# Attention scores of a fused trunk: the product of the rotated queries with the low part of the rotated keys on 64 rows of the array, two key banks from different row halves

## What is computed

```python
def mla_attend(q_n, q_r, k_n, k_r, v):
    s = jnp.einsum('bqhd,bkhd->bhqk', q_n, k_n) + jnp.einsum('bqhr,bkr->bhqk', q_r, k_r)
    p = jax.nn.softmax(s.astype(jnp.float32) * MLA_SCALE, axis=-1)
    return jnp.einsum('bhqk,bkhd->bqhd', p.astype(v.dtype), v)
...
    qr_l = apply_rope(qr_l, cos[:, None, :], sin[:, None, :])
    ...
    y_lat = (o_lat * jax.nn.silu(s_lat[3])) @ w_out
```

## Time and profile before

| | us |
|---|---|
| median of three runs | 3075.17 |
| lowest and highest | 3072.52, 3076.87 |
| the profiled execution's own time | 3071.61 |
| its span (first to last instruction) | 3069.8 |
| TensorE busy in it | 2917.5 (95%) |
| attention stage, from its first loads to its last matmul | about 1869 to 2857 |

### The profile page before, as it was taken

How to read it: one execution, slowest core, us unless ns; L and a number is a source line. 1 busy time by engine, 2 the same in 40 slices (tenths; PEclk the granted TensorE clock), 3 DMA queues, 4 the chain that set the end, 5 groups by cost and what they waited for, 6 DMA issues and landing times. The chain is left out here.

```text
span 3069.8 us, 38485 instructions
## 1 busy us (share of the span) xinstructions
PE 2917.5 (95%) x15623; PEld 2505.9 (82%) x15623; DVE 1531.2 (50%) x2791; ACT 1178.5 (38%) x1971; POOL 234.9 (8%) x275
## 2 busy tenths in 40 slices
PE   7999999999999999979979997999999999999798
PEld 7788888888888788857867886888888888887577
DVE  2625652654365535544432323666666656665353
ACT  2423322331233123322234222666666666665310
POOL 0100000000000000002320000202102012020000
PEclk8899999999999999989989998999999999999799
DMA  6311131113111311153341221000100101100432
GB/s 187 93 33 44 45 114 30 44 52 107 30 46 50 107 30 52 33 204 108 121 146 39 90 96 46 26 28 26 32 25 26 36 18 32 31 19 18 175 110 69
DMA packets 223866, 200.79 MB, mean 65 GB/s; under 512 B 12141, under 2 KB 194301, under 8 KB 223690
## 3 DMA queue, kind: packets, MB, share of 16 engines
q1 hardware_dynamic: 207194, 171.28, 18.5%
q0 software_dynamic: 4656, 16.56, 1.4%
q10 hardware_dynamic: 11840, 10.49, 1.0%
HBM read 157.34 MB, written 40.95 MB: 65 GB/s over the span
## 5 line engine op out<-in xcount | busy, mean ns | idle before, releaser
L40 PE MATMUL v_pj<-e_u_hi,e_w_hi 128*128 128x512 f32 (+1 forms) x864 | 308.7, 357 | 1.9 <-PEq L57 1.9
L40 PE MATMUL v_pj<-e_u_hi,v_w_hi 128*128 128x512 f32 (+1 forms) x864 | 308.6, 357 | 0.0
L41 PE MATMUL v_pj<-e_u_lo,v_w_hi 128*128 128x512 f32 (+1 forms) x864 | 306.7, 355 | 0.0
L41 PE MATMUL v_pj<-e_u_lo,e_w_hi 128*128 128x512 f32 (+1 forms) x864 | 306.7, 355 | 0.0
L42 PE MATMUL v_pj<-e_u_hi,v_w_lo 128*128 128x512 f32 (+1 forms) x864 | 306.5, 355 | 0.0
L42 PE MATMUL v_pj<-e_u_hi,e_w_lo 128*128 128x512 f32 (+1 forms) x864 | 306.5, 355 | 0.0
L40 PE MATMUL o_y_bank<-o_w_hi,o_m_hi 128*128 128x512 f32 x576 | 230.9, 401 | 48.8 <-DVE o_w_lo L1218 31.2
L1840 ACT CAST t_pt_hi<-t_ring 128x512 fp32r<-128x512 f32 (+1 forms) x384 | 181.6, 519 | 237.3 <-PE t_ring L2024 237.3
L1925 DVE TENSOR_TENSOR t_pt_lo<-t_ring,t_pt_hi 128x512 fp32r<-128x512 f32 (+1 forms) x384 | 216.2, 598 | 52.8 <-ACT t_pt_hi L1840 51.4
L41 PE MATMUL o_y_bank<-o_w_lo,o_m_hi 128*128 128x512 f32 x576 | 229.0, 398 | 0.0
L42 PE MATMUL o_y_bank<-o_w_hi,o_m_lo 128*128 128x512 f32 x576 | 228.6, 397 | 0.0
(11 more groups left out here) (380 smaller groups left out, 6446.5 us busy)
## 6 DMA issues: line engine op xcount, KB each, us to landing
e_w_raw<-in_ev_w_in SPq DMA_DIRECT2D x72, 512.0 KB, 4.7
v_mw<-in_mod_w SPq DMA_DIRECT2D x32, 512.0 KB, 4.3
l_w_raw<-in_od_w_in SPq DMA_DIRECT2D x21, 512.0 KB, 4.0
o_m_raw<-mixT SPq DMA_DIRECT2D x20, 512.0 KB, 5.3
m_w<-in_mod_w SPq DMA_DIRECT2D x16, 512.0 KB, 7.7
o_w_raw<-in_ev_w_out SPq DMA_DIRECT2D x16, 512.0 KB, 10.3
zgT<-l_lat_q POOLq DMA_DIRECT2D x16, 512.0 KB, 3.6
t_zg<-zgT SPq DMA_DIRECT2D x32, 256.0 KB, 2.7
```

Of the source, the lines that this page charges most:

```text
L40: nc.tensor.matmul(out, whi, xhi, start=first, stop=False)
L41: nc.tensor.matmul(out, whi, xlo, start=False, stop=False)
```

## The change

It does four things.

1. In `scores` the matmul with `kr2[1]` no longer takes 128 rows. It takes the high half alone, 64 rows; low x low is left out. Bank 1 takes it from rows (64 to 127) and banks 2 and 0 from rows 0 to 63. The three matmuls stand together behind bank 1's other four: bank 2, bank 1, bank 0 (the last with `start`, so that bank 0's four other matmuls add to it).
2. The high part must then lie in both row halves. A new tile `qx` holds a copy in the half that `qs` doesn't have it in. GpSimd makes the copy (`other_half`, 64 x 1024) in t = 5 of the head before, and for head 0 ahead of the slots; TensorE waits for it (`qx_ok`) in t = 0 of each head, just ahead of these three matmuls.
3. `zg` is one tile instead of two. The second half's gates are loaded when the first half's store has landed, and the next head's first half when the second's has.
4. `part` is no tile of its own but the first 512 columns of `w_raw`; the load of an even head's key weights into `w_raw` also waits for the turned queries (`turn_ok`).

```diff
         qs = [s.sb(f"qs{b}", [P, LAT], F32R) for b in range(2)]
+        qx = s.sb("qx", [P, LAT], F32R)
...
-        zg = [s.sb(f"zg{x}", [P, 512]) for x in range(2)]
-        turn, part = s.sb("turn", [P, LAT]), s.sb("part", [P, 512])
+        zg = s.sb("zg", [P, 512])
+        turn, part = s.sb("turn", [P, LAT]), w_raw[:, 0:512]
...
                 if n > 4:
                     sp.wait_ge(w_ok, n - 1)
+                    if (kind, h % 2) == ("k", 0):
+                        sp.wait_ge(turn_ok, h)
...
-                if h + 1 < AH:
-                    sp.wait_ge(og_out[x], 16 * (h + 1))
-                    gates(h + 1, x)
+                if (h, x) != (AH - 1, 1):
+                    sp.wait_ge(og_out, 16 * (2 * h + x + 1))
+                    gates(h + x, 1 - x)
...
+            def other_half(h):
+                r = DR * (h % 2)
+                o = DR - r
+                pool.wait_ge(qs_hi_ok, h + 1)
+                pool.tensor_copy(qx[o:o + DR, :], f(qs[h % 2][r:r + DR, :])).then_inc(qx_ok, 1)
+
             add(0, 0)
             add(0, 1)
+            other_half(0)
             for h, t in slots:
                 for op in projections(h, t):
                     if op[0] == "qr":
                         add(op[1], op[2])
+                if t == 5 and h + 1 < AH:
+                    other_half(h + 1)
...
+                hi_rows = [slice(DR * g, DR * g + DR) for g in range(2)]
+                high = [(qs[b] if g == b else qx)[hi_rows[g], tok] for g in range(2)]
+
+                def rope_low(j, g):
+                    k0, n = KEYS[j]
+                    return nc.tensor.matmul(S[:, k0:k0 + n], high[g], kr2[1][hi_rows[g], k0:k0 + n], start=j == 0, stop=j != 0)
+
                 for j in SCORE_ORDER:
                     k0, n = KEYS[j]
                     out = S[:, k0:k0 + n]
-                    mm3(nc, out, (qn[b][0][:, tok], qn[b][1][:, tok]), (kn[b][0][:, k0:k0 + n], kn[b][1][:, k0:k0 + n]), True, False)
-                    nc.tensor.matmul(out, qs[b][:, tok], kr2[0][:, k0:k0 + n], start=False, stop=False)
-                    last = nc.tensor.matmul(out, qs[b][:, tok], kr2[1][:, k0:k0 + n], start=False, stop=True)
+                    mm3(nc, out, (qn[b][0][:, tok], qn[b][1][:, tok]), (kn[b][0][:, k0:k0 + n], kn[b][1][:, k0:k0 + n]), j != 0, False)
+                    last = nc.tensor.matmul(out, qs[b][:, tok], kr2[0][:, k0:k0 + n], start=False, stop=j == 0)
                     if j == 1:
-                        last.then_inc(qk_part, 1)
+                        if t == 0:
+                            pe.wait_ge(qx_ok, h + 1)
+                        rope_low(2, 0)
+                        rope_low(1, 1).then_inc(qk_part, 1)
+                        rope_low(0, 0)
                 last.then_inc(qk_done, 1)
```

More of the change, by code:

```diff
@@ L1702, in stage_attend @@
             "qk_part", "qk_done", "most_ok", "bias_ok", "exp_ok", "rec_ok", "prob_ok"))
-        rope_part, rope_own = s.sem("rope_part"), s.sem("rope_own")
+        rope_part, rope_own, qx_ok = s.sem("rope_part"), s.sem("rope_own"), s.sem("qx_ok")
         turn_ok, qs_hi_ok, qs_ok = s.sem("turn_ok"), s.sem("qs_hi_ok"), s.sem("qs_ok")
-        zg_in, og_out = [s.sem(f"zg_in{x}") for x in range(2)], [s.sem(f"og_out{x}") for x in range(2)]
+        zg_in, og_out = s.sem("zg_in"), s.sem("og_out")
         wq_src = a["od_w_uq"].rearrange("a (k p) n -> p (a k) n", p=P)
@@ L1760, in gates @@
             def gates(h, x):
-                sp.dma_start(zg[x][:, :], zg_src[h * P:h * P + P, 512 * x:512 * x + 512]).then_inc(zg_in[x], 16)
+                sp.dma_start(zg[:, :], zg_src[h * P:h * P + P, 512 * x:512 * x + 512]).then_inc(zg_in, 16)
             def store(h, x):
                 sp.wait_ge(ring_free, at[("PV", h, x)])
-                sp.dma_start(og_dst[h * P:h * P + P, 512 * x:512 * x + 512], zg[x][:, :]).then_inc(og_out[x], 16)
-                if h + 1 < AH:
-                    sp.wait_ge(og_out[x], 16 * (h + 1))
-                    gates(h + 1, x)
+                sp.dma_start(og_dst[h * P:h * P + P, 512 * x:512 * x + 512], zg[:, :]).then_inc(og_out, 16)
+                if (h, x) != (AH - 1, 1):
+                    sp.wait_ge(og_out, 16 * (2 * h + x + 1))
+                    gates(h + x, 1 - x)
             for kind, h in LOADS[:4]:
@@ L1772, in _ @@
             gates(0, 0)
-            gates(0, 1)
             for h, t in slots:
@@ L1782, in _ @@
             store(AH - 1, 1)
-            for x in range(2):
-                sp.wait_ge(og_out[x], 16 * AH)
+            sp.wait_ge(og_out, 16 * 2 * AH)
         @block.gpsimd
@@ L1915, in low @@
                     dve.wait_ge(ring_done, at[op])
-                    dve.wait_ge(zg_in[x], 16 * (h + 1))
-                    nc.vector.scalar_tensor_tensor(zg[x][:, :], ps[:, :], 0.5, zg[x][:, :], ALU.mult, ALU.mult).then_inc(ring_free, frees(op))
+                    dve.wait_ge(zg_in, 16 * (2 * h + x + 1))
+                    nc.vector.scalar_tensor_tensor(zg[:, :], ps[:, :], 0.5, zg[:, :], ALU.mult, ALU.mult).then_inc(ring_free, frees(op))
                 else:
```

## The result

The changed kernel takes 3090.99 us in the median of 4 runs (3089.47 to 3096.77). The kernel before takes 3074.06 us beside it (4 runs, 3072.52 to 3076.87). The ratio is 1.0058, with a 95% interval of 1.004 to 1.0075: slower by 16.9 us, by more than the 0.2% that a measurement here can tell. The forecast was 3088.0 with a range of 3071 to 3120, and slower at 0.70. The profiled execution has a span of 3087.7 us, 17.9 over the 3069.8 of before.

The account below looks back on a forecast made before the run. The prediction took TensorE, busy 95% of the span, as the bound. It added 12.8 us (128 x 0.10) for the slots and 0.5 for GpSimd to 3075.2, giving 3088 us, range 3071 to 3120.

Parts of the forecast that it names:

- The mechanism: TensorE's score block: row halves overlap, but each row change empties the array (0.09 us) and exposes a load; +0.10 us per slot.
- the 0.23 us that the overlap saves: TensorE's low-key matmuls: bank 1's runs beside those of banks 2 and 0, 0.35 us replacing 0.58 per slot.
- The rival without overlap: Rival: crossings are paid and the row halves do not run side by side; +0.33 us per slot, 42 us, 3117; chance 0.19.
- the one without a crossing price: Rival: the halves overlap and row changes cost nothing; 128 x 0.23 us gained, 3046; chance 0.16.
- neither: Rival: 64 rows are treated like 128, loads hidden, nothing side by side; 3075; chance 0.09.
- the load on the way in: First 64-row weight load after the 128-row matmuls: 0.03 us exposed, taken from the 36-row matmuls at 164 us.
- the estimate by the page: Weight load into 64 rows, by the skill's rule that rows don't count: 0.08 us more per slot, 10 us in all.
- those slots cost the same: Slots whose scores wait for exponentials: a block ending 0.10 us later shifts that chain as much.
- The 12.8 + 0.5: The forecast's sum: 128 x 0.10 us for TensorE's slots plus 0.5 us for GpSimd's copy, 13.3 us.
- the 0.5 for GpSimd: GpSimd's copy, priced at 1.3 to 2.4 us and expected second behind VectorE, its wait covered: 0.5 us allowed.
- the 14 us in the range: If GpSimd's copy gets in before VectorE's L1931: 1.7 us in head 0 and 12 us over the other 15 heads.
- Buffers and SyncE's waits: One gate tile, part in w_raw and SyncE's added waits: expected to cost nothing.

Follow-up runs that it names:

- e3: The changed kernel with all three 64-row low-key matmuls in one row half, so none can run beside another: 3117.08 us, ratio 1.0149 to the kernel before.
- e4: The kernel before, each low-key matmul in its old place but over 64 rows, three crossings there and back per slot: 3221.13 us, ratio 1.0485.
- e2: The changed kernel with the three low-key matmuls at their new place but over all 128 rows: 3076.49 us, ratio 1.0011 to the kernel before.
- e7: The kernel before, low-key matmuls over 128 rows but 64 columns, ahead of the high-key ones, three times a slot: 3071.92 us, ratio 0.9995.
- e6: The changed kernel with the short matmuls over 32 rows instead of 64: 3090.05 us, ratio 1.0052 to the kernel before.
- e5: The changed kernel with short matmuls on 64 x 64 tiles, ahead of the high-key matmuls of banks 2 and 1: 3086.46 us, ratio 1.004.
- e8: The kernel before with VectorE's split of the key weights moved behind the next slot's maximum: 3066.55 us, ratio 0.9982.
- e10: The changed kernel with a write of 64 zeros on VectorE ahead of its turned low halves, so GpSimd's copy starts first: 3091.29 us.
- e9: The changed kernel with GpSimd's copy waiting for VectorE's turned low halves instead of ScalarE's high halves: 3099.72 us.
- E1: The kernel before with only one gate tile, part in w_raw and SyncE's new waits: 3072.97 us, ratio 1.000.

## Why the prediction was right, point by point

**The mechanism.** It holds in all its parts. A load at a change of rows is held until 0.08 to 0.09 us after the columns ahead of it are in, and nothing hides that load. The halves run side by side (e3). The same gap and an unhidden load come again on the way back. That the array empties in those 0.08 to 0.09 us is my name for the gap. The runs show its size and that it comes with a change of rows, not what the load waits for. The fork between the rivals was whether a way there and back costs more or less than the 0.23 us that the overlap saves. It costs 0.40. The rival without overlap fell with the timeline of after and with e3, the one without a crossing price with e4, and "neither" with the change's own ratio beside that of e2. The reason that spoke for no crossing price, rows 8, was a true row of another kind: e7 shows that going to 64 columns is free. The 2-column tiles of rows 7 did show the gap of 0.09; what sets them apart from 64 columns (the width, or the plain fp32 data) wasn't tried.

The Trainium skill ("TensorEngine Tiling (Array Packing)", section "Key Properties") says that changing the tiling mode drains the array. The change, e4 and e6 agree for the rows, with 0.09 us each way. E7 does not: 128 x 128 to 128 x 64 and back shows no drain in 768 changes. By the page e7 would have cost at least 768 x 0.09 = 69 us, an estimate that uses the gap measured here. The measurement decides.

The Trainium skill ("TensorE: Matmul & The Clock Gate", section "Part 3: Packing small matmuls — row/col tiling") has matmuls of different row groups start some 4 ns apart. The matmuls of the two halves here are printed with starts 0.01 us apart (2111.74 and 2111.75), as their loads are, and 0.01 us is the grain of the timeline. The trace agrees as far as it can.

**The term that was mis-sized: the load on the way in.** The prediction put the first short matmul 0.32 + 0.03 = 0.35 us behind the last long one; it is 0.31 + 0.10 = 0.41. Bank 0's came at 0.54 instead of 0.47, the next load at 0.86 instead of 0.79, the next long one at 0.97 instead of 0.90. All the later steps carry the same 0.07 us and no error of their own. 0.03 was what the 36-row matmuls of rows 5 had shown. I took it for an effect of the few rows. E6 refutes that: 32 rows expose 0.10. What differs is the kind of matmul. Those of rows 5 are transposes, with the identity as an input, of plain fp32 data. The loads of the trace of before, by name: count, ns min/median/max, first and last start. First the 36-row tiles, then the 128-row transposes of the probabilities, then a product of plain fp32 data that is no transpose:

```profile
L984 PEld LDWEIGHTS v_x<-k_ident,e_gate_i x10: 138/139/143, 164.0 to 164.6; 36*128 36x128 f32 x10
...
L2024 PEld LDWEIGHTS t_ring<-k_ident,t_prob x1280: 138/140/231, 1902.9 to 2845.5; 128*128 128x128 f32 x183
...
L1620 PEld LDWEIGHTS l_ss<-l_sq,l_ones x24: 187/188/338, 1607.3 to 1675.7; 128*128 128x128 f32 x24
```

Both transposes take 0.14 us, one with 36 rows and one with 128. The loads of the scores take 0.18 to 0.19 us with 32, 64 and 128 rows, and the plain fp32 product takes as long as they do. So the duration goes with being a transpose, and not with the rows or the number format. Why transposes load faster wasn't tried. Nor does the duration alone give the exposed part: the loads of 64 columns in e5 print 0.13 us and expose 0.05, those of rows 5 print 0.14 and expose 0.03.

Here the Trainium skill ("TensorE: Matmul & The Clock Gate", section "LDWEIGHTS (loading the stationary operand)") was right and my reading of the row was wrong. It says that the rows don't count, and the prediction worked out 10 us more by it. Measured are 0.10 us exposed with 32 rows and with 64, and the estimate by the page was nearer for this step than mine.

**The step that was wrong: "those slots cost the same".** By the timeline 0.17 to 0.19 us a slot would be 22 to 24 us, and the span grew by 17.9. Most of the difference is in the slots where TensorE waits for exponentials. I had written that a later block shifts that chain as much. In head 15 it does: TensorE waits 1.34, 1.43, 1.34 and 1.34 us ahead of t = 3, 4, 5 and 7 both before and after. In two other kinds of slot it doesn't. The wait that TensorE has ahead of the scores in three kernels, in the order before, after and e8. Columns: us in total, times, longest.

```profile
PE t_scores L40 <- ACT t_prob L1851: 16.1, 21, 2.0
...
PE t_scores L40 <- ACT t_prob L1861: 12.6, 21, 1.8
...
PE t_scores L40 <- ACT t_prob L1851: 9.8, 7, 2.0
```

After waits 3.5 us less than before, as often. Most of it, 2.8 us, goes in t = 7 of even heads and t = 0 of odd ones. The timeline of before, head 2, t = 7:

```profile
2066.69 0.69 DVE L1923 SCALAR_TENSOR_TENSOR t_qn_lo<-t_ring,t_qn_hi 128x512 fp32r<-128x512 f32 x1 [1.00 <-ACT t_qn_hi L1838]
...
2067.30 0.68 DVE L1895 TENSOR_TENSOR t_wk_lo<-t_w_raw,t_wk_hi 128x512 fp32r<-128x512 f32 x1
...
2067.90 0.95 DVE L1937 TENSOR_REDUCE t_most<-t_scores 128x1 f32<-128x768 f32 x1
...
2069.67 1.33 ACT L1851 ACTIVATE t_prob<-t_scores,t_bias 128x1280 f32<-128x1280 f32 x1 [0.91 <-DVE t_bias L1941]
...
2071.23 0.35 PE L40 MATMUL t_scores<-t_kn_hi,t_qn_hi 128*128 128x256 f32 x1 [0.37 <-ACT t_prob L1851]
```

and the same place after:

```profile
2069.54 0.69 DVE L1933 SCALAR_TENSOR_TENSOR t_qn_lo<-t_ring,t_qn_hi 128x512 fp32r<-128x512 f32 x1 [1.00 <-ACT t_qn_hi L1848]
...
2070.14 0.68 DVE L1905 TENSOR_TENSOR t_wk_lo<-t_w_raw,t_wk_hi 128x512 fp32r<-128x512 f32 x1
...
2070.74 0.95 DVE L1947 TENSOR_REDUCE t_most<-t_scores 128x1 f32<-128x768 f32 x1
...
2074.08 0.36 PE L40 MATMUL t_scores<-t_kn_hi,t_qn_hi 128*128 128x256 f32 x1 [0.16 <-ACT t_prob L1861]
```

The maximum starts without a pause behind the split in both, so it doesn't start when its scores are ready but when VectorE is through with L1923 and the key weights. The chain hangs on VectorE, not on the block, and a block longer by 0.19 us only eats TensorE's wait: 0.37 became 0.16. The slot lasts 6.58 us before and 6.57 after; an odd head's t = 0 lasts 6.84 in both. There are 14 such slots, seven of each kind (head 14's t = 7 and head 15's t = 0 have no split). They changed by -0.1 us together, so they took in 14 x 0.19 + 0.1 = 2.8 us. Head 14's t = 7 grew by 0.20 us like any other. Head 15's t = 0 went from 6.17 to 5.96 us and so took in 0.4 more, for a reason that no run here shows. Together that makes some 3.1 us.

E8 tests this: with the split behind the maximum the wait should go. Its timeline, where these scores start at 2064.99 and those of before at 2064.65:

```profile
2067.02 0.69 DVE L1923 SCALAR_TENSOR_TENSOR t_qn_lo<-t_ring,t_qn_hi 128x512 fp32r<-128x512 f32 x1 [1.00 <-ACT t_qn_hi L1838]
2067.63 0.95 DVE L1937 TENSOR_REDUCE t_most<-t_scores 128x1 f32<-128x768 f32 x1
...
2069.28 0.68 DVE L1895 TENSOR_TENSOR t_wk_lo<-t_w_raw,t_wk_hi 128x512 fp32r<-128x512 f32 x1
...
2071.05 0.28 PE L40 MATMUL t_scores<-t_kn_hi,t_qn_hi 128*128 128x256 f32 x1
```

The scores of the next slot no longer wait, and the slot is 6.06 us instead of 6.58. In the profiles these 14 slots give 8.5 us, in the medians the kernel gains 6.7; e8's profile loses 1.6 of the 8.5 again in head 15, t = 1, at the lower clock told under e2.

**The account.** The starts of the scores give the growth of each slot, in 127 distances from one slot's scores to the next. 109 of them grew by 0.14 to 0.22 us, 20.4 us together. The 14 absorbing slots gave -0.1 and head 15's t = 0 gave -0.2. In head 0, t = 0 and 1 didn't grow, and t = 2 was 1.4 us shorter. The stretches there, before and then after (the last figures are the granted clock, the DMA share and GB/s):

```profile
1906.00:1910.00 4.00, 3.61 (x12) 3.00 (x13) 1.73 (x4) 2.35 (x5) 0.00 (x0) 0.64 0.00 0
```

```profile
1907.00:1911.00 4.00, 3.70 (x20) 2.78 (x21) 2.48 (x5) 2.26 (x5) 0.00 (x0) 1.00 0.00 0
```

The score block of this one slot ran at 2.4 GHz rather than largely at 1.2 (3.17 us, not 4.57). The full clock is there in e10's profile too (1.00 from 1906 to 1912 us), but not in e9's (0.72 from 1914 to 1920). A stretch that comes and goes like this is no gain of the change that I can show. The sum over the 127 distances is +18.7 us, and the first scores start 0.9 us later. The span's +17.9 leaves -1.7 us behind the last scores. There too the clock differs: over the 70 us from the last slot's first score matmul on, its mean is 0.78 before and 0.85 after, with 0.80 in e10 and 0.78 in e9, and after's stretch behind the last scores is the shortest of these.

With 0.10 in place of 0.03 and the absorbing slots the forecast's sum would have been 128 x 0.17 - 3.1 = 18.7 us. That this is the measured sum to the tenth is luck: the 109 slots grew by 0.19 us each rather than 0.17 (0.01 of it is in e2 as well), and head 0 gave as much back. The 12.8 + 0.5 that I gave came near the 16.9 of the medians in part by luck too. The load was priced 9 us too low, the slots that absorb were priced 3.1 us too high, the 0.5 for GpSimd isn't found, and this profile is 1.6 us shorter by the clock in head 0 and 1.7 us shorter behind the last scores.

**GpSimd's copy: 0.5 us taken, none found.** The order of the two engines came as foreseen: VectorE is first by 0.03 us, GpSimd waits, and its cover takes that. The copy ends at 1894.42, and bank 1's short matmul reads it from 1896.45 on, 2.0 us of cover in head 0 and more elsewhere. Two numbers were off. The price of 1.3 to 2.4 us bounded a copy that takes 1.04 alone. And the 14 us in the range, for the case that GpSimd gets in first, were far too many: e10 is that case, and its price is 0.9 us in head 0 and nothing in the other 15. VectorE's instruction grew by 0.75 us there, not by the 1.76 of rows 11. That row was no price for one copy: behind L1152 stood a second GpSimd instruction, so that both L1214 had one beside them, each over 128 rows where the copy has 64:

```profile
1445.22 3.26 POOL L1154 TENSOR_TENSOR o_h_out<-o_h_out,o_ln_b 128x1024 f32<-128x1024 f32 x1
```

The slack that I had put at 0.5 us plus a few tenths was enough for it.

The Trainium skill ("SBUF — State Buffer", section "Who interferes with whom") says that a VectorE instruction with two inputs in SBUF contends with a GpSimd instruction that reads SBUF, and that the order of issue decides which one is blocked. After, e9 and e10 agree: 2.09 against 1.04 us for the copy, and 1.97 against 1.22 for VectorE's instruction when it comes second.

**Buffers and SyncE's waits: nothing.** E1 shows it, at 1.000 [0.999, 1.001].

## What to carry to other kernels

Row tiles side by side pay only if what runs beside one another is longer than the way there and back, here 0.23 us gained against 0.40 paid. So collect many short products between two crossings (not tried here), or leave them at full height, where the weight loads are hidden. Before pricing a step by a row from elsewhere in the trace, look whether the row is of the same kind: 0.03 against 0.10 us came from taking a transpose's load for a product's. And in a slot with a wait, ask what the chain hangs on before saying that it shifts along; if it is another engine's queue, look at the order of that queue, which here was worth 6.7 us (e8).

## What the hardware showed that I had not expected

- At a granted clock of 1.00 a weight load takes 0.18 to 0.19 us with 32, 64 and 128 rows, but 0.13 with 64 columns (e5, e7), and 0.14 in transposes.
- Going between 128 x 128 and 128 x 64 tiles is free, 768 times over (e7). Going between 128 rows and 64 or 32 costs about 0.40 us there and back.
- Loads of the two row halves start 0.01 us apart and both take 0.18 us.
- GpSimd's copy of 64 x 1024 elements takes 1.04 us alone and 2.09 when it starts 0.03 us behind a VectorE instruction with two SBUF inputs. A start order of hundredths of a microsecond decides who pays (e9, e10). So a duration read beside another engine's work need not be a price.
